# Prompt attention of a streaming encoder step: masking on GpSimd, plain transposes, outputs normalised by queries

## The chip, the core and the metric

The kernel runs on one core of a Trainium2 chip. The time is the device time of one execution in microseconds (us). The core's engines work side by side: TensorE (PE; PEld is its weight load), VectorE (DVE), ScalarE (ACT), GpSimd (POOL) and SyncE (SP), which here issues the loads and stores. Each engine runs its own list of instructions in order, and they meet only at semaphores.

## The reference, cut to what matters

The program is one inference step of a two-layer encoder for one prompt of 512 rows and eight running streams of 16 new rows. The part of interest is the first layer's attention over the prompt, eight heads of 64 columns, with a bias made of a running sum c of forget values:

```python
def fox_block(q, k, v, cq, ck, qpos, kpos):
    s = jnp.einsum('bqhd,bkhd->bhqk', q, k).astype(jnp.float32) * (HEAD_DIM ** -0.5)
    bias = jnp.swapaxes(cq, 1, 2)[..., :, None] - jnp.swapaxes(ck, 1, 2)[..., None, :]
    mask = kpos[None, :] <= qpos[:, None]
    p = jax.nn.softmax(jnp.where(mask, s + bias, -jnp.inf), axis=-1)
    return jnp.einsum('bhqk,bkhd->bqhd', p.astype(v.dtype), v)

def fox_prompt(q, k, v, logf):
    ...
    for i in range(t_len // Q_BLOCK):
        lo, hi = i * Q_BLOCK, (i + 1) * Q_BLOCK
        outs.append(fox_block(q[:, lo:hi], k[:, :hi], v[:, :hi], c[:, lo:hi], c[:, :hi], pos[lo:hi], pos[:hi]))
```

A block of 128 queries sees the keys up to its own end; only the last 128 of these keys need the mask. The streams' attention (the same over 512 cached keys and 16 new ones, for each of eight streams) follows, then the layer's RWKV heads, and the feed-forward parts stand before and behind.

## The kernel before

The engines' lists are written by hand, one function per engine and stage, and called in a fixed order: no scheduler moves anything. Prompt attention is `pe_prompt`, `dve_prompt` and `act_prompt`, with `sp_streams` and `pool_streams` (loads and operands of the streams' attention) beside it.

There are 16 steps. `pstep(n)` gives step n its pair of heads p = n // 4 and its tile of 128 queries qt = n % 4; the step has kl = 128 (qt + 1) keys, so the steps of a pair grow: 128, 256, 384, 512 keys. Scores are negated (q is scaled by a negative factor), so that the row minimum plays the part of the maximum. A step goes through these operations, for both heads of the pair (h = 0, 1):

- `scores` (TensorE, L1154): queries times keys into banks b and b + 1 of PSUM, then (L1157) a product of the identity and `causal` (0 or 1e30) added to the last 128 columns.
- `biased` (VectorE, L1110): adds `c_rows`, the forget sums of the pair's heads as rows that stand on all partitions, writes `prob` and the row minimum `nmax`. `c_rows` lies in `norm_buf`, 512 columns for each head.
- `exponentials` (ScalarE, L1083): in place, with the row sums into `esum`.
- `diagonals` (VectorE, L1118, L1120): the reciprocal of the sums, and the identity times it (`sum_diag`).
- `turn` (TensorE, L1167): each 128x128 block of `prob` times `sum_diag`, which turns and normalises it, into banks 4 and 5. ScalarE copies head 0 (L1101) and VectorE head 1 (L1143) to `prob_t` in `pair_raw`.
- `outputs` (TensorE, L1179): v of one head as weights (64 columns) times the turned block (128 columns), summed over the key blocks. The result has the head's columns on partitions and the queries on columns, in bank 6 or 7.
- ScalarE rounds it into `act_hi` (L1092), VectorE writes the rest into `act_lo` (L1136). These are the operands of the output projection.

The loops interleave the steps. In iteration n TensorE issues `scores(n + 1)`, `outputs(n - 1)`, `turn(n)`; ScalarE `act_hi` of n - 1, `exponentials(n + 1)`, the copy of n; VectorE `biased(n + 1)`, `act_lo` of n - 1, the copy of n, `diagonals(n + 1)`. `prob` has two buffers, `prob_t` one.

The streams' attention begins once the last `act_lo` is written (`s_ol`). Its cached keys and values are loads of 1 MB, with two buffers each: the first lies in `yflat`, the second in `norm_buf`, keys on the forget rows of heads 0 to 3, values on those of heads 4 to 7. `sp_streams` issues the first stream's loads early, waits for the last `act_lo`, issues the second stream's, then the RWKV stage's loads (`sp_rwkv_loads`), and then for each further stream its keys, when the keys of two streams before have been turned (L1231), and its values, when the products of two streams before are done. GpSimd's `pool_streams` clears and fills `q_blocks` (on the same memory as `head_rows`) and copies the new keys while the prompt's steps run.

Of the kernel before, what the change touches and what calls it, by code (L numbers as in the profile page):

```python
# [157 lines left out]
def build(nc, io):  # L158
    ctx = ExitStack()
    with ctx:  # L160
# [114 lines left out]
        sum_diag = [pair_raw[0][:, 4 + 2 * i:6 + 2 * i, :] for i in range(2)]  # L275
# [10 lines left out]
        def level_mask(lv):  # L286
# [60 lines left out]
        s_sc, s_bs, s_ex, s_rs, s_dg = (sem(n) for n in (  # L347
            "scores", "scores_with_bias", "exponentials", "row_sum_inverse", "sum_diagonals"))
# [722 lines left out]
        def pstep(n):  # L1071

            p, qt = divmod(n, 4)
            return p, qt, (qt + 1) * P, 2 * (n % 2)

        def act_prompt(act):
            def exponentials(n):
                p, qt, kl, b = pstep(n)
                for h in range(2):
                    act.wait_ge(s_bs, 2 * n + h + 1)  # L1080
                    if n >= 2:
                        act.wait_ge(s_dg, n - 1)
# [5 lines left out]
            for n in range(PSTEPS + 1):  # L1088
                if n >= 1:
                    p, qt, kl, b = pstep(n - 1)  # L1090
                    act.wait_ge(s_o, n)
                    act.activation(act_hi[:, p, qt * P:(qt + 1) * P], ps[:, 6 + (n - 1) % 2, 0:P], ACT.Copy)\  # L1092
                       .then_inc(s_oh, 1)
# [9 lines left out]
        def dve_prompt(dve):  # L1103
            def biased(n):
                p, qt, kl, b = pstep(n)
                for h in range(2):
                    dve.wait_ge(s_sc, 2 * n + h + 1)
                    if n >= 2:
                        dve.wait_ge(s_pt, 2 * (n - 1))
# [5 lines left out]
            def diagonals(n):  # L1115
                b = pstep(n)[3]
                dve.wait_ge(s_ex, 2 * n + 2)
                dve.reciprocal(rsum[:, b:b + 2], esum[:, b:b + 2]).then_inc(s_rs, 1)  # L1118
                dve.wait_ge(s_rs, n + 1)
                dve.tensor_tensor(sum_diag[n % 2], ident[:, :].rearrange("p (o c) -> p o c", o=1)  # L1120
                                  .broadcast_to([P, 2, P]),
                                  rsum[:, b:b + 2].rearrange("p (h o) -> p h o", o=1).broadcast_to([P, 2, P]),
                                  ALU.mult).then_inc(s_dg, 1)
# [4 lines left out]
            diagonals(0)  # L1128
            for n in range(PSTEPS + 1):
                if n + 1 < PSTEPS:  # L1130
                    biased(n + 1)
                if n >= 1:
                    p, qt, kl, b = pstep(n - 1)
                    cols = slice(qt * P, (qt + 1) * P)
                    dve.wait_ge(s_oh, n)
                    dve.tensor_tensor(act_lo[:, p, cols], ps[:, 6 + (n - 1) % 2, 0:P],  # L1136
                                      act_hi[:, p, cols].bitcast(F32), ALU.subtract).then_inc(s_ol, 1)
                if n < PSTEPS:
# [4 lines left out]
                    dve.tensor_copy(prob_t[1][:, 0:kl], ps[:, 5, 0:kl]).then_inc(s_ptd, 1)  # L1143
                if n + 1 < PSTEPS:
                    diagonals(n + 1)

        def pe_prompt(pe):
            def scores(n):
# [3 lines left out]
                for h in range(2):  # L1152
                    rows = slice(64 * h, 64 * h + 64)
                    pe.matmul(ps[:, b + h, 0:kl], qk[rows, p, qt * P:(qt + 1) * P], qk[rows, 4 + p, 0:kl],  # L1154
                              start=True, stop=False)
                for h in range(2):
                    pe.matmul(ps[:, b + h, qt * P:kl], ident[:, :], causal, start=False, stop=True)\  # L1157
                      .then_inc(s_sc, 1)

            def turn(n):  # L1160
                p, qt, kl, b = pstep(n)
                pe.wait_ge(s_dg, n + 1)
                for h in range(2):
# [262 lines left out]

# [1486 lines left out]
```

## Time and profile before

| | us |
|---|---|
| median of 3 runs | 2772.81 (2771.42 to 2778.17) |
| the profiled execution | 2770.99 |
| its span | 2769.2 |
| TensorE busy | 2649.7 (96%) |
| VectorE busy | 1031.3 (37%) |
| ScalarE busy | 889.2 (32%) |
| GpSimd busy | 97.0 (4%) |

The span is what the profiler recorded of that execution, and the execution's own time lies 1.8 us above it. The steps of prompt attention are a small part of it, so shares over the span say little about them; they are read from the table of stretches and from the instructions in order of time. In a row of the timeline the first number is the start in us from the span's start, the second how long the merged instructions take together; "[... <-X]" is idle time of the engine ahead of it and who ended it. An f32 product shows as two records; a transpose of one 128x128 block as one.

### The profile page before, as it was taken

The page shows a single profiled execution, that of the slowest core. Times are in us where ns is not written, and L with a number is a line of the kernel's source. Part 1 is how long each engine was busy: PE and PEld are TensorE (multiplying, and loading weights), DVE is VectorE, ACT ScalarE, POOL GpSimd, SP SyncE. Part 2 cuts the span into 40 slices and gives each one's busy share as a digit, 9 for nine tenths or more (in the row PEclk, how much of TensorE's full clock was granted, in tenths as well). Part 3 has the DMA queues.
Part 4 walks back from the last instruction along what each step waited for, and adds up shares of the span by engine and source line. Part 5 has one row for each costly group of instructions (what it writes and reads, how often), then busy time and mean ns, then how long its engine had stood idle before and what let it go on. Part 6 is the DMA issues. An engine that isn't in the chain of part 4 may idle for free. (4 is left out here: it accounts for less than half of the span.)

```text
span 2769.2 us, 46298 instructions
## 1 busy us (share of the span) xinstructions
PE 2649.7 (96%) x19617; PEld 2414.5 (87%) x19617; DVE 1031.3 (37%) x1387; ACT 889.2 (32%) x1517; POOL 97.0 (4%) x88
## 2 busy tenths in 40 slices
PE   7999999999987988999999999999999989999998
PEld 7998997998656876899899899989979769989997
DVE  3232224332534764522232352222243364222234
ACT  4331223222334554432122343212233344321222
POOL 0000001000001221000000100000010010000001
PEclk9999999999899999999999999999999999999999
DMA  4221222221261003222222222312223222222222
GB/s 129 76 87 58 76 68 84 76 68 52 74 204 55 3 5 94 60 76 78 74 76 76 84 71 74 95 60 74 70 75 100 69 61 73 71 87 65 76 76 84
DMA packets 279809, 208.66 MB, mean 75 GB/s; under 512 B 24292, under 2 KB 236414, under 8 KB 279688
## 3 DMA queue, kind: packets, MB, share of 16 engines
q1 hardware_dynamic: 279688, 206.91, 24.9%
q8 instruction: 92, 1.51, 0.2%
q14 instruction: 29, 0.24, 0.0%
HBM read 199.85 MB, written 7.03 MB: 75 GB/s over the span
## 5 line engine op out<-in xcount | busy, mean ns | idle before, releaser
L449 PE MATMUL ps<-act_hi,pair_hi 128*128 128x320 f32 x2976 | 678.5, 309 | 0.6 <-DVE pair_lo L411 0.6
L449 PE MATMUL ps<-act_lo,pair_hi 128*128 128x320 f32 x2976 | 678.4, 309 | 0.0
L449 PE MATMUL ps<-act_hi,pair_lo 128*128 128x320 f32 x2976 | 677.3, 309 | 0.0
L449 PEld LDWEIGHTS ps<-act_hi,pair_lo 128*128 128x128 f32 x2976 | 497.8, 188 | 0.0
L449 PEld LDWEIGHTS ps<-act_lo,pair_hi 128*128 128x128 f32 x2976 | 497.8, 188 | 0.0
L449 PEld LDWEIGHTS ps<-act_hi,pair_hi 128*128 128x128 f32 x2976 | 496.7, 188 | 0.8 <-ACT qk L890 0.8
L411 DVE TENSOR_TENSOR pair_lo<-pair_raw,pair_hi 128x1024 fp32r<-128x1024 f32 x206 | 253.7, 1236 | 425.6 <-ACT pair_hi L407 425.6
L407 ACT ACTIVATE pair_hi<-pair_raw 128x1024 fp32r<-128x1024 f32 x206 | 215.9, 1053 | 457.6 <-PE ps L449 310.6
L485 PE MATMUL ps<-row_hi,hid_hi 128*128 128x512 f32 x880 | 345.8, 393 | 6.7 <-DVE row_lo L438 6.7
L485 PE MATMUL ps<-row_hi,hid_lo 128*128 128x512 f32 x880 | 344.4, 391 | 0.0
L485 PE MATMUL ps<-row_lo,hid_hi 128*128 128x512 f32 x880 | 344.3, 391 | 0.0
L430 ACT ACTIVATE row_hi<-row_raw 128x512 fp32r<-128x512 f32 x228 | 141.6, 630 | 404.3 <-DMA row_raw<-in_ffn_w_out_dram 274.0
L438 DVE TENSOR_TENSOR row_lo<-row_raw,row_hi 128x512 fp32r<-128x512 f32 x228 | 168.4, 752 | 247.6 <-ACT row_hi L430 247.1
L605 ACT ACTIVATE hid_hi<-hid 128x640 f32 (+1 forms) x88 | 65.1, 740 | 538.5 <-DVE hid L632 538.5
L632 DVE TENSOR_TENSOR hid<-silu,ps 128x640 f32<-128x640 f32 x88 | 72.3, 821 | 422.9 <-PE ps L449 413.1
L485 PEld LDWEIGHTS ps<-row_hi,hid_hi 128*128 128x128 f32 x880 | 165.1, 188 | 44.3 <-DVE row_lo L438 8.6
L485 PEld LDWEIGHTS ps<-row_lo,hid_hi 128*128 128x128 f32 x880 | 165.1, 188 | 36.8
L485 PEld LDWEIGHTS ps<-row_hi,hid_lo 128*128 128x128 f32 x880 | 165.2, 188 | 35.6
L485 PE MATMUL ps<-row_hi,act_hi 128*128 128x512 f32 x280 | 116.4, 416 | 17.6 <-DVE row_lo L438 16.6
L469 PE MATMUL ps<-act_hi,pair_hi 128*128 128x320 f32 x320 | 101.7, 318 | 18.5 <-DVE act_lo L749 13.0
L795 POOL TENSOR_TENSOR y<-y,norm_buf 128x512 f32<-128x512 f32 x30 | 44.1, 1504 | 2047.6 <-ACT norm_buf L676 2047.6
L485 PE MATMUL ps<-row_lo,act_hi 128*128 128x512 f32 x280 | 113.3, 405 | 0.0
(383 smaller groups left out, 2562.8 us busy)
## 6 DMA issues: line engine op xcount, KB each, us to landing
pair_raw<-in_ffn_w_in_dram SPq DMA_DIRECT2D x176, 512.0 KB, 3.8
row_raw<-in_ffn_w_out_dram SPq DMA_DIRECT2D x176, 256.0 KB, 2.9
pair_raw<-in_even_w_in_dram SPq DMA_DIRECT2D x22, 512.0 KB, 3.8
norm_buf<-in_norm_g_dram SPq DMA_DIRECT2D x12, 512.0 KB, 4.3
y<-in_cache_fox_k_dram SPq DMA_DIRECT2D x4, 1024.0 KB, 7.6
y<-in_cache_fox_v_dram SPq DMA_DIRECT2D x4, 1024.0 KB, 6.7
norm_buf<-in_cache_fox_k_dram SPq DMA_DIRECT2D x4, 1024.0 KB, 7.7
norm_buf<-in_cache_fox_v_dram SPq DMA_DIRECT2D x4, 1024.0 KB, 5.4
```

The source lines that it names most:

```text
L407: act.activation(pair_hi[c][:, :, :], pair_raw[c][:, :, :], ACT.Copy).then_inc(s_pair_hi[c], 1)
L411: dve.tensor_tensor(pair_lo[c][:, :, :], pair_raw[c][:, :, :], pair_hi[c][:, :, :].bitcast(F32), ALU.subtract).then_inc(s_pair_lo[c], 1)
L430: act.activation(row_hi[i % n][:, :], raw, ACT.Copy).then_inc(s_row_hi, 1)
L438: dve.tensor_tensor(row_lo[i % n][:, :], raw, row_hi[i % n][:, :].bitcast(F32), ALU.subtract).then_inc(s_row_lo, 1)
L449: mm = pe.matmul(ps[:, 2 * c + h, 0:HALF], w[c][:, k, :], a[:, k, h * HALF:(h + 1) * HALF], start=(k == 0 and w is pair_hi and a is act_hi ...
L469: mm = pe.matmul(ps[:, 2 * c + h, 0:HALF], w[c][:, k, :], a[:, k, h * HALF:(h + 1) * HALF], start=(k == 0 and w is pair_hi and a is act_hi ...
L485: mm = pe.matmul(ps[:, bank, :], a[:, k, t * P:(t + 1) * P], w[i % n][:, :], start=(k == 0 and w is row_hi and a is left_hi), stop=(k == k ...
L605: act.activation(halves(hid_hi, j), hid[:, :, :], ACT.Copy).then_inc(s_hid_hi, 1)
L632: dve.tensor_tensor(hid[:, :, :], silu[:, :, :], wide(2), ALU.mult).then_inc(s_pair_read[1], 1)
L795: pool.tensor_tensor(y[:, t, 0:512], y[:, t, 0:512], g_post[:, 0:512], ALU.mult).then_inc(s_yg[0], 1)
```

## The change

**Masking.** The two mask products of each step are gone. GpSimd adds `causal` to the last 128 columns of the pair's forget rows, in place, before the step's `biased` reads them. So that the mask may stay there, a pair's query tiles run from the last to the first: 512, 384, 256, 128 keys. Each mask but a pair's first waits until the previous step's bias has been added, and `biased` waits for it (`s_mask`). The streams' operands are made between masks.

**Turning.** `turn` is a plain transpose of each block and waits for the exponentials, not for a diagonal. `sum_diag` is gone; `inverse` only takes the reciprocal.

**Outputs.** The turned block is now the weights (128 columns) and v of one head streams (64 columns); the result has the queries on partitions. VectorE multiplies it by the reciprocal sums (`normalised`, into `fox_out`), TensorE transposes that (`turn_out`) into the same bank's next 128 columns, and from there `act_hi` and `act_lo` are read. VectorE's `act_lo` now stands behind its copy of the turned probabilities.

**Loads.** The second stream's keys wait for eight steps of bias (`s_bs` at 16), its values for all sixteen (32), not for the last `act_lo`.

```diff
@@ pstep @@
-            return p, qt, (qt + 1) * P, 2 * (n % 2)
+            return p, 3 - qt, (4 - qt) * P, 2 * (n % 2)
@@ act_prompt @@
                     if n >= 2:
-                        act.wait_ge(s_dg, n - 1)
+                        act.wait_ge(s_rs, n - 1)
...
-                    act.wait_ge(s_o, n)
-                    act.activation(act_hi[:, p, qt * P:(qt + 1) * P], ps[:, 6 + (n - 1) % 2, 0:P], ACT.Copy)\
+                    act.wait_ge(s_ot, n)
+                    act.activation(act_hi[:, p, qt * P:(qt + 1) * P], ps[:, 6 + (n - 1) % 2, P:2 * P], ACT.Copy)\
                        .then_inc(s_oh, 1)
@@ dve_prompt @@
                     dve.wait_ge(s_sc, 2 * n + h + 1)
+                    dve.wait_ge(s_mask, n + 1)
...
-            def diagonals(n):
+            def inverse(n):
                 b = pstep(n)[3]
                 dve.wait_ge(s_ex, 2 * n + 2)
+                if n >= 2:
+                    dve.wait_ge(s_on, n - 1)
                 dve.reciprocal(rsum[:, b:b + 2], esum[:, b:b + 2]).then_inc(s_rs, 1)
+
+            def normalised(n):
+                b = pstep(n)[3]
+                dve.wait_ge(s_o, n + 1)
                 dve.wait_ge(s_rs, n + 1)
-                dve.tensor_tensor(sum_diag[n % 2], ident[:, :].rearrange("p (o c) -> p o c", o=1)
-                                  .broadcast_to([P, 2, P]),
-                                  rsum[:, b:b + 2].rearrange("p (h o) -> p h o", o=1).broadcast_to([P, 2, P]),
-                                  ALU.mult).then_inc(s_dg, 1)
+                if n >= 2:
+                    dve.wait_ge(s_ot, n - 1)
+                dve.tensor_tensor(fox_out[n % 2].rearrange("p (h c) -> p h c", h=2),
+                                  ps[:, 6 + n % 2, 0:P].rearrange("p (h c) -> p h c", h=2),
+                                  rsum[:, b:b + 2].rearrange("p (h o) -> p h o", o=1).broadcast_to([P, 2, HEAD]),
+                                  ALU.mult).then_inc(s_on, 1)
...
                 if n >= 1:
-                    p, qt, kl, b = pstep(n - 1)
...
+                    normalised(n - 1)
                 if n < PSTEPS:
...
                     dve.tensor_copy(prob_t[1][:, 0:kl], ps[:, 5, 0:kl]).then_inc(s_ptd, 1)
+                if n >= 1:
+                    lo(n - 1)
                 if n + 1 < PSTEPS:
-                    diagonals(n + 1)
+                    inverse(n + 1)
@@ pe_prompt @@
                     pe.matmul(ps[:, b + h, 0:kl], qk[rows, p, qt * P:(qt + 1) * P], qk[rows, 4 + p, 0:kl],
-                              start=True, stop=False)
-                for h in range(2):
-                    pe.matmul(ps[:, b + h, qt * P:kl], ident[:, :], causal, start=False, stop=True)\
-                      .then_inc(s_sc, 1)
+                              start=True, stop=True).then_inc(s_sc, 1)
...
-                pe.wait_ge(s_dg, n + 1)
                 for h in range(2):
+                    pe.wait_ge(s_ex, 2 * n + h + 1)
                     if n:
                         pe.wait_ge(s_ptd if h else s_pta, n)
                     for k in range(qt + 1):
-                        mm = pe.matmul(ps[:, 4 + h, k * P:(k + 1) * P], prob[n % 2][h][:, k * P:(k + 1) * P],
-                                       sum_diag[n % 2][:, h, :], start=True, stop=True)
+                        mm = pe.transpose(ps[:, 4 + h, k * P:(k + 1) * P], prob[n % 2][h][:, k * P:(k + 1) * P],
+                                          ident[:, :])
...
-                for k in range(qt + 1):
-                    for h in range(2):
-                        mm = pe.matmul(ps[64 * h:64 * h + 64, 6 + n % 2, 0:P],
-                                       vtok[:, k, p * P + 64 * h:p * P + 64 * h + 64],
-                                       prob_t[h][:, k * P:(k + 1) * P], start=(k == 0), stop=(k == qt))
+                for h in range(2):
+                    for k in range(qt + 1):
+                        mm = pe.matmul(ps[:, 6 + n % 2, 64 * h:64 * h + 64], prob_t[h][:, k * P:(k + 1) * P],
+                                       vtok[:, k, p * P + 64 * h:p * P + 64 * h + 64], start=(k == 0), stop=(k == qt))
                 mm.then_inc(s_o, 1)
+
+            def turn_out(n):
+                pe.wait_ge(s_on, n + 1)
+                pe.transpose(ps[:, 6 + n % 2, P:2 * P], fox_out[n % 2], ident[:, :]).then_inc(s_ot, 1)
...
                 if n < PSTEPS:
                     turn(n)
+                if n >= 1:
+                    turn_out(n - 1)
@@ sp_streams @@
                 if b == 1:
-                    sp.wait_ge(s_ol, PSTEPS)
+                    sp.wait_ge(s_bs, PSTEPS)
...
+                if b == 1:
+                    sp.wait_ge(s_bs, 2 * PSTEPS)
@@ pool_streams, now pool_prompt_and_streams @@
+            def mask(n):
+                p, qt, kl, b = pstep(n)
+                if n % 4:
+                    pool.wait_ge(s_bs, 2 * n)
+                if n % 4 == 0:
+                    pool.wait_ge(s_cra, p + 1)
+                    pool.wait_ge(s_crd, p + 1)
+                at = c_rows[:, 2 * p:2 * p + 2, qt * P:kl]
+                pool.tensor_tensor(at, at, same(causal, 2), ALU.add).then_inc(s_mask, 1)
```

The masks stand in GpSimd's list as 0 to 3, the clearing of `q_blocks`, 4 and 5, four of its copies (head 0), 6, four more (head 1), 7 and 8, the two copies of the new keys and forget values, 9 to 15.

TensorE, inside a pair: scores of the next step, outputs of the step before, turning of this step (here one with 384 keys in both). Before:

```order
L1154 MATMUL ps<-qk 128x512 [waits scores_with_bias]
L1154 MATMUL ps<-qk 128x512
L1157 MATMUL ps<-att_const,ident 128x128 x2
L1179 MATMUL ps<-pair_raw,vtok 64x128 [waits fox_lo,prob_t_by_dve,prob_t_by_act]
L1179 MATMUL ps<-pair_raw,vtok 64x128 x3
L1167 MATMUL ps<-pair_raw,xn_buf 128x128 [waits prob_t_by_act,sum_diagonals]
L1167 MATMUL ps<-pair_raw,xn_buf 128x128 x2
L1167 MATMUL ps<-pair_raw,xn_buf 128x128 [waits prob_t_by_dve]
L1167 MATMUL ps<-pair_raw,xn_buf 128x128 x2
```

TensorE at the same place now (L1169 scores, L1191 outputs, L1179 turning, L1197 the output's transpose):

```order
L1169 MATMUL ps<-qk 128x256 [waits scores_with_bias]
L1169 MATMUL ps<-qk 128x256
L1191 MATMUL ps<-vtok,pair_raw 128x64 [waits fox_lo,prob_t_by_dve,prob_t_by_act]
L1191 MATMUL ps<-vtok,pair_raw 128x64 x7
L1179 MATMUL ps<-ident,xn_buf 128x128 [waits prob_t_by_act,exponentials]
L1179 MATMUL ps<-ident,xn_buf 128x128 x2
L1179 MATMUL ps<-ident,xn_buf 128x128 [waits prob_t_by_dve,exponentials]
L1179 MATMUL ps<-ident,xn_buf 128x128 x2
L1197 MATMUL ps<-ident,pair_raw 128x128 [waits fox_normalised]
```

The mask products are gone, outputs have the form 128x64, and behind the turning stands a transpose of the outputs of the step before.

ScalarE, two iterations in the first pairs (L1092 act_hi, L1083 exponentials, L1101 the copy of turned probabilities). Before:

```order
L1092 ACTIVATE act_hi<-ps 128x128 [waits fox_out]
L1083 ACTIVATE xn_buf,esum<-xn_buf,nmax 128x384 [waits sum_diagonals,scores_with_bias] x2
L1101 ACTIVATE pair_raw<-ps 128x256 [waits fox_out,prob_turned]
L1092 ACTIVATE act_hi<-ps 128x128 [waits fox_out]
L1083 ACTIVATE xn_buf,esum<-xn_buf,nmax 128x512 [waits sum_diagonals,scores_with_bias] x2
L1101 ACTIVATE pair_raw<-ps 128x384 [waits fox_out,prob_turned]
```

ScalarE now:

```order
L1093 ACTIVATE act_hi<-ps 128x128 [waits fox_turned]
L1084 ACTIVATE xn_buf,esum<-xn_buf,nmax 128x256 [waits row_sum_inverse,scores_with_bias] x2
L1102 ACTIVATE pair_raw<-ps 128x384 [waits fox_out,prob_turned]
L1093 ACTIVATE act_hi<-ps 128x128 [waits fox_turned]
L1084 ACTIVATE xn_buf,esum<-xn_buf,nmax 128x128 [waits row_sum_inverse,scores_with_bias] x2
L1102 ACTIVATE pair_raw<-ps 128x256 [waits fox_out,prob_turned]
```

The order of the three is the same; `act_hi` waits for the output's transpose instead of the outputs.

SyncE's queue at the second stream's loads (keys, values, then the first of the RWKV loads). Before:

```order
L1216 DMA y<-in_cache_fox_v_dram 128x4x512
L1212 DMA norm_buf<-in_cache_fox_k_dram 128x4x512 [waits fox_lo]
L1216 DMA norm_buf<-in_cache_fox_v_dram 128x4x512
L1493 DMA rw_const<-in_rw_const_dram 128x836 [waits qk_new_set]
L1494 DMA reset_p<-in_rw_const_dram 128x512
```

The same place now:

```order
L1235 DMA y<-in_cache_fox_v_dram 128x4x512
L1229 DMA norm_buf<-in_cache_fox_k_dram 128x4x512 [waits scores_with_bias]
L1235 DMA norm_buf<-in_cache_fox_v_dram 128x4x512 [waits scores_with_bias]
L1529 DMA rw_const<-in_rw_const_dram 128x836 [waits qk_new_set]
L1530 DMA reset_p<-in_rw_const_dram 128x512
```

Nothing moved in the queue; the two waits are for bias steps instead of the last `act_lo`.

## Rows read from the trace of the kernel before

**Rows 1.** Table of stretches: pair 1 and pair 3 of prompt attention; columns in the head line.

```profile
core 0: us, PE busy (x) PEld busy (x) DVE busy (x) ACT busy (x) POOL busy (x), PEclk, DMA share, GB/s
715.60:731.65 16.05, 16.05 (x104) 11.88 (x104) 8.53 (x34) 7.57 (x27) 3.03 (x11) 0.82 0.01 2
745.21:758.77 13.56, 13.56 (x113) 10.15 (x112) 8.57 (x32) 6.85 (x24) 0.00 (x0) 1.00 0.01 2
```

**Rows 2.** Timeline at the stage's end: a copy, the outputs behind it, the streams' first products.

```profile
768.65 0.47 ACT L1101 ACTIVATE pair_raw<-ps 128x384 f32<-128x384 f32 x1
...
769.25 0.88 PE L1179 MATMUL ps<-pair_raw,vtok 128*64 128x128 f32 x12 [0.70 <-ACT pair_raw L1101]
...
774.72 1.96 PE L1231 MATMUL ps<-ident,y 128*128 128x128 f32 x16 [0.69 <-DVE act_lo L1136]
```

**Rows 3.** Timeline of TensorE alone inside pair 3 (start, us, what).

```profile
751.10 1.13 PE L1154 MATMUL ps<-qk 64*128 64x512 f32 x4
752.16 0.71 PE L1157 MATMUL ps<-att_const,ident 128*128 128x128 f32 x4
752.80 0.66 PE L1179 MATMUL ps<-pair_raw,vtok 128*64 128x128 f32 x8
753.39 1.60 PE L1167 MATMUL ps<-pair_raw,xn_buf 128*128 128x128 f32 x12
754.92 0.49 PE L1154 MATMUL ps<-qk 64*128 64x128 f32 x4
755.35 0.71 PE L1157 MATMUL ps<-att_const,ident 128*128 128x128 f32 x4
...
756.79 2.05 PE L1167 MATMUL ps<-pair_raw,xn_buf 128*128 128x128 f32 x16
758.77 0.49 PE L1154 MATMUL ps<-qk 64*128 64x256 f32 x2
```

**Rows 4.** Timeline of TensorE in the streams' attention: third, fourth and fifth key turn.

```profile
797.09 1.97 PE L1231 MATMUL ps<-ident,y 128*128 128x128 f32 x8 [5.78 <-DMA y<-in_cache_fox_k_dram]
...
806.11 1.09 PE L1231 MATMUL ps<-ident,norm_buf 128*128 128x128 f32 x8
...
814.17 1.09 PE L1231 MATMUL ps<-ident,y 128*128 128x128 f32 x8 [0.28 <-DMA y<-in_cache_fox_k_dram]
```

**Rows 5.** Timeline of SyncE's queue: second stream's values, RWKV states, third stream's keys.

```profile
775.11 0.51 SPq L1216 DMA_DIRECT2D norm_buf<-in_cache_fox_v_dram  x1
...
779.51 9.78 SPq L1501 DMA_DIRECT2D state_raw<-in_state_rwkv_dram  x8
789.34 0.62 SPq L1212 DMA_DIRECT2D y<-in_cache_fox_k_dram  x1
```

**Rows 6.** Lines L1003 (transposes) and L2447 (one streamed column): ns min/median/max, first and last start.

```profile
L1003 PE MATMUL ps<-ident,qk x20: 272/273/302, 690.3 to 692.4; 128*128 128x128 f32 x20
```

```profile
L2447 PE MATMUL ps<-ones,ln_g x16: 245/245/266, 2152.0 to 2153.7; 1*128 1x1 f32 x16
```

**Rows 7.** Timeline of ScalarE inside pair 3.

```profile
753.51 0.28 ACT L1092 ACTIVATE act_hi<-ps 128x128 fp32r<-128x128 f32 x1 [1.64 <-PE ps L1179]
753.68 0.71 ACT L1083 ACTIVATE xn_buf<-xn_buf,nmax 128x512 f32<-128x512 f32 x1
...
755.09 0.48 ACT L1101 ACTIVATE pair_raw<-ps 128x384 f32<-128x384 f32 x1
...
757.08 0.39 ACT L1083 ACTIVATE xn_buf<-xn_buf,nmax 128x128 f32<-128x128 f32 x1
...
757.99 0.60 ACT L1101 ACTIVATE pair_raw<-ps 128x512 f32<-128x512 f32 x1
```

**Rows 8.** Groups of GpSimd, shapes apart: busy us, mean ns, idle before.

```profile
L2304 POOL TENSOR_TENSOR norm_buf<-norm_buf,rw_const 128x512 f32<-128x512 f32 x8 | 10.2, 1273 | 54.7 <-DVE norm_buf L2134 46.4 <-PE ps L1781 4.4 <-DVE sig_g L1559 3.9
```

**Rows 9.** Table of stretches behind the late key load, and in the streams' last steps.

```profile
797.10:800.00 2.90, 2.90 (x14) 2.90 (x15) 0.21 (x1) 0.65 (x3) 0.00 (x0) 0.50 1.05 387
800.00:801.00 1.00, 1.00 (x10) 0.85 (x8) 0.64 (x3) 0.81 (x1) 0.00 (x0) 1.00 0.28 102
851.00:854.30 3.30, 1.49 (x17) 1.11 (x17) 2.26 (x9) 0.94 (x4) 0.00 (x0) 1.00 0.00 0
```

More of the change, by code:

```diff
@@ L274, in build @@
         prob_t = [pair_raw[h][:, 0:4, :].rearrange("p k c -> p (k c)") for h in range(2)]
-        sum_diag = [pair_raw[0][:, 4 + 2 * i:6 + 2 * i, :] for i in range(2)]
+        fox_out = [pair_raw[0][:, 4 + i, :] for i in range(2)]
         new_mask = yflat[:, 4096:5120].rearrange("p (b c) -> p b c", c=P)
@@ L346, in build @@
         s_cr, s_cra, s_crd = sem("c_rows"), sem("c_rows_by_act"), sem("c_rows_by_dve")
-        s_sc, s_bs, s_ex, s_rs, s_dg = (sem(n) for n in (
-            "scores", "scores_with_bias", "exponentials", "row_sum_inverse", "sum_diagonals"))
+        s_sc, s_bs, s_ex, s_rs, s_mask, s_on, s_ot = (sem(n) for n in (
+            "scores", "scores_with_bias", "exponentials", "row_sum_inverse", "diagonal_masked", "fox_normalised",
+            "fox_turned"))
         s_pt, s_pta, s_ptd, s_o, s_oh, s_ol = (sem(n) for n in (
@@ L1113, in biased, with lo @@
                                              accum_out=nmax[:, b + h:b + h + 1]).then_inc(s_bs, 1)
-            def diagonals(n):
+            def inverse(n):
                 b = pstep(n)[3]
                 dve.wait_ge(s_ex, 2 * n + 2)
+                if n >= 2:
+                    dve.wait_ge(s_on, n - 1)
                 dve.reciprocal(rsum[:, b:b + 2], esum[:, b:b + 2]).then_inc(s_rs, 1)
+            def normalised(n):
+                b = pstep(n)[3]
+                dve.wait_ge(s_o, n + 1)
                 dve.wait_ge(s_rs, n + 1)
-                dve.tensor_tensor(sum_diag[n % 2], ident[:, :].rearrange("p (o c) -> p o c", o=1)
-                                  .broadcast_to([P, 2, P]),
-                                  rsum[:, b:b + 2].rearrange("p (h o) -> p h o", o=1).broadcast_to([P, 2, P]),
-                                  ALU.mult).then_inc(s_dg, 1)
+                if n >= 2:
[4 more added lines that the diff above has]
+                                  ALU.mult).then_inc(s_on, 1)
+            def lo(n):
+                p, qt, kl, b = pstep(n)
+                cols = slice(qt * P, (qt + 1) * P)
+                dve.wait_ge(s_oh, n + 1)
+                dve.tensor_tensor(act_lo[:, p, cols], ps[:, 6 + n % 2, P:2 * P],
+                                  act_hi[:, p, cols].bitcast(F32), ALU.subtract).then_inc(s_ol, 1)
             dve.wait_ge(s_cra, FOXH // 2)
@@ L1127, in dve_prompt @@
             biased(0)
-            diagonals(0)
+            inverse(0)
             for n in range(PSTEPS + 1):
@@ L1132, in dve_prompt @@
                 if n >= 1:
-                    p, qt, kl, b = pstep(n - 1)
[L1134 to L1137, printed above, removed]
+                    normalised(n - 1)
                 if n < PSTEPS:
@@ L1408, in pool_fox_setup, with pool_prompt_and_streams, q_blocks_of @@
                                pattern=[[-FOXH, NSEQ], [-1, FOXH], [0, NEW]], channel_multiplier=1).then_inc(s_sel, 1)
-        def pool_streams(pool):
-            for c in range(2):
-                pool.wait_ge(s_pair_read[c], before("even_in", 0) + NQK + NRW + 1)
-            pool.wait_ge(s_cr, FOXH)
-            pool.memset(q_blocks, 0.0).then_inc(s_qb0, 1)
-            pool.wait_ge(s_qb0, 1)
-            for h in range(2):
+        def pool_prompt_and_streams(pool):
+            def mask(n):
+                p, qt, kl, b = pstep(n)
+                if n % 4:
[5 more added lines that the diff above has]
+                pool.tensor_tensor(at, at, same(causal, 2), ALU.add).then_inc(s_mask, 1)
+            def q_blocks_of(h):
                 rows = slice(64 * h, 64 * h + 64)
@@ L1420, in pool_streams @@
                                      qk[rows, p, SEQ:TOK].rearrange("p (b q) -> p b q", q=NEW)).then_inc(s_qb0, 1)
+            pool.wait_ge(s_att_const, 16)
+            for n in range(4):
+                mask(n)
+            for c in range(2):
+                pool.wait_ge(s_pair_read[c], before("even_in", 0) + NQK + NRW + 1)
+            pool.memset(q_blocks, 0.0).then_inc(s_qb0, 1)
+            mask(4)
+            mask(5)
+            pool.wait_ge(s_qb0, 1)
+            pool.wait_ge(s_mask, 6)
+            q_blocks_of(0)
+            pool.wait_ge(s_qb0, 5)
+            mask(6)
+            pool.wait_ge(s_mask, 7)
+            q_blocks_of(1)
             pool.wait_ge(s_qb0, 9)
+            mask(7)
+            mask(8)
             pool.wait_ge(s_logf, 1)
@@ L1425, in pool_streams @@
             pool.tensor_copy(k_new, qk[:, 4:8, SEQ:TOK]).then_inc(s_qkn, 1)
+            for n in range(9, PSTEPS):
+                mask(n)
         F4 = lambda a: a.rearrange("p (k c) -> p k c", k=4)
@@ L2759, in _ @@
             pool_fox_setup(pool)
-            pool_streams(pool)
+            pool_prompt_and_streams(pool)
             pool_rwkv_first(pool)
```

## The prediction

> **What bounds the kernel now.** The page shows one core with TensorE busy for 96% of 2769.2 us, so the first reading is where the edited work stands. By the table of stretches the sixteen steps of prompt attention begin at 715.60 us and the streams' attention at 774.72 [rows 1, 2]: 59.1 us of the span. In the middle, four steps (one pair of heads) take 13.56 us, and TensorE is busy for all of it, VectorE for 8.57 and ScalarE for 6.85 [rows 1]. TensorE's own rows have no idle note and follow each other without a gap: scores of 512 keys 1.06 us from start to start, the two mask products 0.64, outputs 0.59, turning 384 probabilities 1.53, turning 512 1.98 [rows 3]. So TensorE bounds this stretch, and the other engines have slack. Behind it the streams' third key load lands late: TensorE stands still for 5.78 us before 797.09 [rows 4]. The load was issued only at 789.34, 14.2 us after the issue at 775.11, with the RWKV loads in between, eight of which alone hold the queue for 9.78 us [rows 5].
>
> **What goes from TensorE.** The mask products: 0.64 us in each of 16 steps, 2.6 us per pair. The turning: between 384 and 512 keys two products more cost 0.45 us, so one f32 product of 128 columns costs 0.225 us and a step about 0.18 us beside it. A pair has 20 of them (two heads times 1+2+3+4 blocks), 20 x 0.225 + 4 x 0.18 = 5.2 us. A plain transpose costs 0.11 us: twenty start within 2.0 us [rows 6]. So 20 x 0.11 + 4 x 0.12 = 2.7 us, 2.5 us less.
>
> **What comes to TensorE.** Outputs by queries load 128 columns of probabilities as weights and stream only 64 columns of v. No row has that shape. Nearest are products with 128 weight columns and one streamed column: 16 records (two to a product) start within 1.7 us, 0.113 us each, as long as with 128 streamed columns [rows 3, 6]. I therefore take 0.225 us for each, 20 x 0.225 + 4 x 0.18 = 5.2 us per pair; before, outputs cost (0.59 us with two blocks) about 0.15 + 0.22 per block, 2.8 us per pair. If the streamed columns alone set the price, it would be half, 3.0 us; if load and product didn't overlap at all, 0.3 us a product, 6.8. I take 5.2, since the weight load is what these rows and the turning rows share. The output's own transpose adds 0.11 us in each step, and about 0.3 until ScalarE can read it. TensorE's own work per pair is then 3.0 (scores, 4 x 0.22 + 0.21 for each block) + 2.7 + 5.2 + 0.9 = 11.8 us in place of 13.56. If it alone bounded the stretch, that would save 7 us.
>
> **Why I don't take that saving.** The edit ties ScalarE into a ring. In its list the rounding copy into act_hi stands ahead of the next exponentials, and it now waits for the transposed output, which TensorE makes only after turning the probabilities. The next outputs wait for the copy that stands behind those exponentials. So from one outputs to the next everything is in series: outputs, turning, output transpose, act_hi, two exponentials, one copy, wake TensorE. Before, ScalarE's copy waited for outputs alone, and its exponentials ran beside the turning. Per pair: outputs 5.2; turning 2.7; output transpose till ScalarE starts 4 x 0.3 = 1.2; act_hi to exponential 4 x 0.17 = 0.7 [rows 7]; exponentials 0.39 us for 128 keys and 0.71 for 512, 0.5 and 0.6 between, two heads, 4.4 [rows 7]; copies 0.60 for 512 keys, 0.48 for 384, 0.37 and 0.26 by the same slope, 1.7 [rows 7]; from a copy's end (768.65 + 0.47) to TensorE's start at 769.25 0.13 us, four times 0.5 [rows 2]. Sum 16.4 us, 2.8 more than 13.56. The next scores lie in the ring's gap and are hidden. VectorE has 8.6 us of work per pair and fits: its normalising (0.3 us) lies beside the turning.
>
> **The end of the stage.** The first outputs start about where they did: scores of 512 and 384 keys at half clock take 3.8 us from 715.6, the first pair's mean granted clock of 0.82 puts the rise near 721 [rows 1], turning ends near 721.4, copy and wake 0.8: 722.4. Three pairs of 16.4 bring 771.6. Three steps to the last outputs are 4.8, 3.8 and 2.3 (a step's share of the ring; the last without 1.4 of exponentials): 782.5. Then the last tile: outputs 0.65, normalise 0.3, transpose 0.3, act_hi 0.3, act_lo 0.3, wake: 784.5. Before it was 774.72 [rows 2]. **The stage loses 9.8 us.**
>
> **GpSimd's masks.** Each adds 2 x 128 columns; a 128x512 addition on GpSimd takes 1.27 us [rows 8], so one takes at most that, probably 0.9. It waits until the previous step's bias has been added and is needed a ring turn later, 3.7 us at the shortest. Ahead of masks 6 and 7 it is queued behind four copies, 1.0 us. I put it at nothing; the cover is gone when mask and queue exceed about 2.4 us.
>
> **The queue of loads.** The second stream's keys now wait for the eighth step's bias and its values for the last step's bias, which come about 8 us ahead of the stage's end, since exponentials, turning, outputs and tail of two small tiles still follow. All that queues behind them moves too: the third key load is issued 14.2 - 8 = 6.3 us after the stage's end instead of 14.6, and lands 7.75 us later (797.09 - 789.34), at 14.1. TensorE wants it at 16.6 (791.31 - 774.72). So the wait of 5.78 goes, with 2.5 us to spare. Behind the wait the clock is 0.50 for 2.9 us [rows 9], and the key turn and its stream last 9.02 us where the next lasts 8.06 [rows 4]: 1.0 more. **Streams gain 6.8 us.** After that the loads set the same beat of 8 us; what is late next is again the key load behind v.
>
> **The sum.** 9.8 - 6.8 = +3.0 us. The profiled execution took 2770.99 us, so the sum gives 2774.0; the median of the runs lies 1.8 above it (2772.81), which gives 2775.8. I say 2775.
>
> **Rivals.** (a) Streamed columns set the price of outputs: the ring is 14.2 us per pair, the stage +1.2, in all -5.6: 2765.4, or 2767 against the median. For it: fewer columns; against it: the one-column products [rows 6]. 0.12. (b) The ring doesn't bind, TensorE's 11.8 us a pair do: stage -7, streams -6.8, 2761. For it: if ScalarE's order let exponentials run ahead; against it: the list in the order shown. 0.07. (c) **Slower by the clock.** TensorE now idles about a quarter of the ring. If the granted clock falls to its lower level inside the stage, the ring's TensorE part (5.2 + 2.7 + 1.2) doubles, 9 us for each pair at half clock; one pair gives 2784, all four 2811. For it: the clock stood at 0.50 behind the 5.78 us stop. Against it: from 851.0 to 854.3 TensorE was busy for 1.49 of 3.30 us at full clock [rows 9], though it dropped afterwards; the ring is busier, without a stop over 1.3 us. It decides from one such drop. The Trainium skill (TensorE: Matmul & The Clock Gate, Part 4) has a rule that speaks for it: transposes don't count as busy for the clock. By it these turns would keep the clock down and this rival would come in. The trace disagrees so far: from 797.1 to 800 TensorE did nothing but transposes at 0.50, and from 800 on the clock was 1.00 [rows 9]. 0.12. (d) The early loads don't bring the third keys forward (SP blocked, landing later): +9.8, 2782 to 2783. The queue rows speak against it [rows 5]. 0.10. (e) The masks don't run ahead and hold VectorE: above 2.4 us each, some 0.5 us a step, 8 in all, 2783. 0.04.
>
> **How the numbers follow.** The forecast has 0.55; its own range is 2770 to 2780, since thirty-two small latencies in the ring may be off by 0.1 us each. About 0.3% (8.3 us) is what a measurement of this kernel can tell from no change: 2764.5 to 2781.1. Faster holds (b) and a little of (a): 0.09. Slower holds (c), (d), (e) and the upper edge of the forecast: 0.27. Within: 0.64. The range goes from 2766 (most of (a)) to 2786 (one pair of (c), outputs at 0.3 us a product); it leaves out (b) and the rest of (c).
>
> **What would show it.** In the changed profile: four steps at 16.4 us with TensorE idle before each outputs, released by ScalarE's copy; outputs at 0.45 us a block of both heads (0.22 refutes me); act_hi waiting for the output transpose; the stage ending near 784.5; no idle before the third key turn; the bias rows never waiting for GpSimd; granted clock 1.00 after 721. A period below 13.6 us would make the prediction wrong from its main step; a clock of 0.50 in the middle would make it wrong upwards.

## The result and the profile after

The changed kernel takes 2790.24 us (median of 4 runs, 2786.89 to 2793.83), the kernel before beside it 2772.45: a ratio of 1.0064, with a 95% interval from 1.0048 to 1.0080. It is slower by 17.8 us, and outside the range of the prediction, 2766 to 2786. The profiled execution took 2787.44 us with a span of 2785.7, 16.5 more than before.

Where the 16.5 us lie, by the starts of three rows (first scores, first key turn, fourth key turn; before 715.60, 774.72, 806.11; after 712.19, 791.46, 818.89): the stage began 3.4 us earlier, lasted 79.3 instead of 59.1 (+20.2), the streams' first three turns took 27.4 instead of 31.4 (-4.0), and all that follows 1966.8 instead of 1963.1 (+3.7).

The table of stretches shows first what went wrong. These are the three parts of the stage behind its first pair in the changed kernel: pair 2, pair 3, and pair 4 with the tail (us, busy time of PE, PEld, DVE, ACT and POOL, then the granted clock). Their counterpart in the kernel before is in [rows 1].

```profile
core 0: us, PE busy (x) PEld busy (x) DVE busy (x) ACT busy (x) POOL busy (x), PEclk, DMA share, GB/s
726.20:742.70 16.50, 12.55 (x81) 8.74 (x80) 8.37 (x33) 6.74 (x24) 5.58 (x14) 0.91 0.05 7
742.70:765.30 22.60, 20.38 (x83) 15.11 (x82) 8.33 (x33) 6.74 (x24) 2.85 (x4) 0.50 0.11 43
765.30:791.46 26.16, 20.61 (x98) 14.37 (x97) 10.60 (x40) 8.77 (x33) 2.17 (x3) 0.63 0.33 104
```

A pair takes 16.5 us at nearly full clock, as the ring's sum said (16.4), and 22.6 at 0.50. A clock of 0.50 in the table is TensorE's lower level (1.2 in place of 2.4 GHz), so the time spent there is twice what a stretch's clock lacks to 1, times its length: 3.0 + 22.6 + 19.4 = 45 us of these 65.

The ring itself, in the timeline of TensorE and ScalarE with the clock at 1.00: outputs, turning, the output's transpose, act_hi, two exponentials, the copy, and the next outputs, which waited 1.30 us for that copy. The scores stand in the gap. In [rows 3, 7] the same operations ran side by side.

```profile
735.94 2.00 PE L1191 MATMUL ps<-vtok,pair_raw 128*128 128x64 f32 x16 [1.41 <-ACT pair_raw L1102]
...
737.78 0.83 PE L1179 MATMUL ps<-ident,xn_buf 128*128 128x128 f32 x6
...
738.44 0.27 PE L1197 MATMUL ps<-ident,pair_raw 128*128 128x128 f32 x1
...
738.64 0.49 PE L1169 MATMUL ps<-qk 64*128 64x128 f32 x4
738.75 0.28 ACT L1093 ACTIVATE act_hi<-ps 128x128 fp32r<-128x128 f32 x1 [2.86 <-PE ps L1197]
738.92 0.50 ACT L1084 ACTIVATE xn_buf<-xn_buf,nmax 128x256 f32<-128x256 f32 x1
...
739.42 0.49 ACT L1084 ACTIVATE xn_buf<-xn_buf,nmax 128x256 f32<-128x256 f32 x1
...
739.91 0.48 ACT L1102 ACTIVATE pair_raw<-ps 128x384 f32<-128x384 f32 x1
...
740.43 1.55 PE L1191 MATMUL ps<-vtok,pair_raw 128*128 128x64 f32 x12 [1.30 <-ACT pair_raw L1102]
```

Eight output products take 1.84 us from their start to the start of what follows (735.94 to 737.78), 0.23 each with 64 streamed columns. That is what f32 products with the same 128 weight columns and 128 streamed ones cost in the kernel before (0.225, turning in [rows 3]), so the streamed columns don't set the price. One pair later the same eight took 3.46 us, at the clock of 0.50:

```profile
754.58 3.67 PE L1191 MATMUL ps<-vtok,pair_raw 128*128 128x64 f32 x16 [0.88 <-ACT pair_raw L1102]
758.04 1.49 PE L1179 MATMUL ps<-ident,xn_buf 128*128 128x128 f32 x6
```

GpSimd's sixteen masks took 0.73 us each and were never late: no bias step waited for one. The timeline row of one, released by the step's bias before it:

```profile
733.41 0.73 POOL L1438 TENSOR_TENSOR norm_buf<-norm_buf,att_const 128x256 f32<-128x256 f32 x1 [1.81 <-DVE nmax L1112]
```

In the streams the wait of [rows 4] is gone. SyncE's queue issued the second stream's values 9.5 us ahead of the stage's end, and the third key turn stood ready; the rows are SyncE's and TensorE's timelines.

```profile
781.91 0.37 SPq L1235 DMA_DIRECT2D norm_buf<-in_cache_fox_v_dram  x1
...
795.16 0.39 SPq L1229 DMA_DIRECT2D y<-in_cache_fox_k_dram  x1
```

```profile
791.46 3.67 PE L1250 MATMUL ps<-ident,y 128*128 128x128 f32 x16 [0.69 <-DVE act_lo L1139]
...
810.67 1.09 PE L1250 MATMUL ps<-ident,y 128*128 128x128 f32 x8
...
818.89 1.09 PE L1250 MATMUL ps<-ident,norm_buf 128*128 128x128 f32 x8 [0.44 <-DMA norm_buf<-in_cache_fox_k_dram]
```

But the streams inherit the low clock: the first key turn takes 3.67 us where it took 1.96 [rows 2], and the third begins 19.2 us after the stage's end, not 16.6.

### The profile page after: what moved, and what is told of

The parts are those of the page before. It is cut to its first block and busy times, and to the rows that moved or that the text cites. A ratio compares the mean times of both kernels' runs of the same rounds, so it can differ in the third digit from the quotient of the medians.

```text
span 2785.7 us, 46113 instructions
## 1 busy us (share of the span) xinstructions
PE 2660.3 (95%) x19489; PEld 2420.7 (87%) x19489; DVE 1029.9 (37%) x1387; ACT 888.2 (32%) x1517; POOL 108.8 (4%) x104
## 5 line engine op out<-in xcount | busy, mean ns | idle before, releaser
L470 PE MATMUL ps<-act_hi,pair_hi 128*128 128x320 f32 x320 | 101.8, 318 | 18.5 <-DVE act_lo L750 13.0
L486 PE MATMUL ps<-row_hi,act_lo 128*128 128x512 f32 x280 | 113.7, 406 | 0.0
```

The source lines that it names most:

```text
L470: mm = pe.matmul(ps[:, 2 * c + h, 0:HALF], w[c][:, k, :], a[:, k, h * HALF:(h + 1) * HALF], start=(k == 0 and w is pair_hi and a is act_hi ...
L486: mm = pe.matmul(ps[:, bank, :], a[:, k, t * P:(t + 1) * P], w[i % n][:, :], start=(k == 0 and w is row_hi and a is left_hi), stop=(k == k ...
```

## The experiments

**Theories.** The ring was measured close to its forecast and the early loads as forecast, so the question is the clock. Three causes were set against each other: the outputs stream only 64 columns behind each weight load (T, thin work); TensorE waits in the ring (I, idle); transposes do not count as work for the clock, as the Trainium skill says (R; TensorE: Matmul & The Clock Gate, Part 4). T+I is the first two together. In the table, the stage is from the first scores to the streams' first key turn, and low clock is 2 x (1 - granted clock) x length, summed over the stage from the second pair on (every kernel starts its first pair at the lower level). The medians are of 10 runs in x3, x4, x6 and x9, 8 in x1, x5 and x8, 4 in the changed kernel and x10, 3 in x7 and 2 in x2. The kernel before ran beside each group and its median moved from 2772.2 to 2775.3, so kernels are best compared by the ratio; it is worked out from all runs and need not be the quotient of two medians. Stage, clock and period are of one profile each.

| kernel | stage us | low clock us | period of pair 3 us | median us | ratio to before (95%) |
|---|---|---|---|---|---|
| before | 59.1 | 0 | 13.56 | | 1 |
| changed | 79.3 | 45 | 22.6 | 2790.24 | 1.0064 (1.0048 to 1.0080) |
| x1 outputs stream 128 columns | 68.0 | 3 | 15.8 | 2778.67 | 1.0023 (1.0011 to 1.0035) |
| x8 filler in the gap | 68.1 | 0 | 16.1 | 2776.22 | 1.0016 (1.0003 to 1.0030) |
| x2 turning by products | 84.1 | 22 | 18.5 | 2787.87 | 1.0054 (1.0034 to 1.0075) |
| x10 transposes twice | 83.9 | 27 | 20.4 | 2793.31 | 1.0053 (1.0034 to 1.0073) |
| x3 exponentials first | 52.6 | 0 | 11.9 | 2765.37 | 0.9984 (0.9969 to 0.9999) |
| x9 exponentials first, 128 columns | 53.1 | 0 | 12.0 | 2760.38 | 0.9954 (0.9941 to 0.9968) |
| x4 early loads alone | 59.9 | 0 | 13.6 | 2767.24 | 0.9978 (0.9963 to 0.9994) |
| x5 masks alone | 55.6 | 0 | 12.3 | 2767.97 | 0.9983 (0.9972 to 0.9995) |
| x6 masks and early loads | 55.1 | 0 | 12.3 | 2764.19 | 0.9965 (0.9951 to 0.9979) |
| x7 changed, late loads | 81.0 | 36 | 16.5 | 2796.40 | 1.0085 (1.0056 to 1.0114) |

**x11, the changed kernel again.** No edit.

> The changed kernel again, for one more profile. If the drop of the clock belongs to the changed stage and not to one execution, it falls to 0.50 for 25 us or more between 720 and 790 again and the stage lasts 76 to 82 us; if it was chance, the stage lasts about 68 us.

One execution, 2791.94 us: stage 81.0 us, 36 us of low clock behind the first pair, nearly all of it in one piece at the end. The place differs from the first profile: there the whole of pair 3, here pair 4 and, before it, the whole first pair (17.9 us at 0.50). Over the whole stage the low clock is 49 us there and 54 here. The table of stretches, pair 3 and the rest:

```profile
747.88:764.34 16.46, 12.44 (x82) 8.63 (x81) 8.25 (x33) 6.73 (x24) 2.85 (x4) 0.91 0.14 55
764.34:794.39 30.05, 24.82 (x98) 18.37 (x97) 10.52 (x40) 8.76 (x33) 2.18 (x3) 0.50 0.35 100
```

So the fall belongs to this stage, not to one execution.

**x1, outputs stream 128 columns.** In `outputs`, with the rows that read it moved along (normalise takes head 0 from columns 0 to 63 and head 1 from 192 to 255, the transpose goes to 384 to 511):

```diff
-                        mm = pe.matmul(ps[:, 6 + n % 2, 64 * h:64 * h + 64], prob_t[h][:, k * P:(k + 1) * P],
-                                       vtok[:, k, p * P + 64 * h:p * P + 64 * h + 64], start=(k == 0), stop=(k == qt))
+                        mm = pe.matmul(ps[:, 6 + n % 2, P * h:P * h + P], prob_t[h][:, k * P:(k + 1) * P],
+                                       vtok[:, k, p * P:p * P + P], start=(k == 0), stop=(k == qt))
```

> Outputs load the same weights but stream both heads' v (128 columns in place of 64; the half that is not wanted is computed and left), which at full clock should cost nothing, since 128 weight columns set the price. In the changed kernel the granted clock fell to 0.50 for 34 us inside the stage, which lasted 79.3 us (712.2 to 791.5). Theory T (thin work: the clock follows how much TensorE streams, and 64 columns behind each weight load are too few): clock 1.00 through pairs 2 to 4, period 16.6 us, stage about 70, total 10 us less. Theory R (transposes do not count as work for the clock) and theory I (TensorE's waits of 1.3 us in the ring lower it): no change, stage 77 to 81.

Outputs of eight products took 1.89 us from start to start (changed: 1.84), the waits stayed, and the clock stayed up through pairs 2 and 3. TensorE's rows, then pair 3 and pair 4 with the tail in the table of stretches:

```profile
750.97 2.05 PE L1194 MATMUL ps<-vtok,pair_raw 128*128 128x128 f32 x16 [1.41 <-ACT pair_raw L1102]
752.86 0.82 PE L1182 MATMUL ps<-ident,xn_buf 128*128 128x128 f32 x6
...
755.51 1.60 PE L1194 MATMUL ps<-vtok,pair_raw 128*128 128x128 f32 x12 [1.30 <-ACT pair_raw L1102]
```

```profile
741.96:757.76 15.80, 11.50 (x82) 8.46 (x81) 8.20 (x33) 6.74 (x24) 2.86 (x4) 1.00 0.16 57
757.76:780.20 22.44, 14.96 (x97) 10.84 (x97) 10.28 (x40) 8.77 (x33) 2.18 (x3) 0.93 0.34 110
```

The streamed columns that nobody reads took 11.3 us off the stage and 11.6 off the median. T is right here; neither I nor R would have it, since waits and transposes are the same. The mean clock over a whole execution says so too: 0.980 to 0.987 in x1's eight runs, 0.974 to 0.978 in the changed kernel's five. But the clock isn't held to the end. In the last 3 us of the stage, from the last outputs on, it fell here as well, and the first key turn took 3.64 us as in the changed kernel.

**x8, filler in the gap.** Ahead of each `outputs`:

```diff
+                    for i in range(4):
+                        pe.matmul(ps[:, 6 + (n - 1) % 2, 3 * P:4 * P], ident[:, :], ident[:, :], start=True, stop=True)
                     outputs(n - 1)
```

> Four products of the identity with itself (128 columns each, 0.9 us in all at full clock, into unused columns of the outputs' bank) stand ahead of each step's outputs, in the stretch where TensorE waits for ScalarE's copy; nothing reads them. If the clock is the missing cost (T or I): clock 1.00, period 16.6 to 17, stage about 70, in spite of more work. If the ring itself was mis-sized and the clock only a companion: stage 79 or more, by up to 0.9 us a step.

```profile
742.47:758.55 16.08, 15.39 (x113) 12.07 (x113) 8.20 (x33) 6.74 (x24) 2.86 (x4) 1.00 0.16 59
```

Sixty-four products more, 14.0 us less in the median: TensorE busy for 15.39 of 16.08 us, clock 1.00, and here up to the streams, whose first key turn took 1.97 us. With the outputs as thin as in the changed kernel, filling the gap is enough too. So it took the two together, thin outputs and idle gaps, and repairing either holds the clock through the pairs. The filler also streams 128 columns a product, so x8 doesn't tell idle time from too little work streamed in all; a single cause of that kind would fit x1 and x8 alike.

**x2, turning by products.** `pe.transpose(..., ident)` becomes `pe.matmul(..., ident, start=True, stop=True)`.

> The probabilities are turned by a product with the identity instead of a transpose (0.225 us a block in place of 0.11, 2.5 us per pair more at full clock); all else as changed. Theory R (transposes do not count): clock 1.00, period 19.0 us, stage about 77. Theory T and theory I: the outputs and the waits stay, so the clock still falls; TensorE's part of the ring at half clock, stage 85 to 95.

**x10, transposes twice.** Each transpose is issued twice into the same place.

> Each block of probabilities is transposed twice into the same place, which takes as long as the product with the identity did (2.2 us per pair more). With products in place of transposes the granted clock was low for 24 us between 727 and 800, where the changed kernel had 51 us. Theory T+I (the clock follows how densely TensorE streams, whatever the kind of work): the same as with products, stage 80 to 88, low clock for 15 to 35 us of it. Theory R (transposes do not count): low throughout as in the changed kernel or more, with TensorE's 14.4 us a pair at half clock, stage 90 or more.

The two take the same time on TensorE (eight blocks 2.00 and 1.91 us) and differ only in the kind of work. Pair 2 and pair 3 of x2, then of x10:

```profile
729.85:749.55 19.70, 16.13 (x101) 12.46 (x100) 8.14 (x32) 6.74 (x24) 5.58 (x14) 0.86 0.04 10
749.55:768.00 18.45, 14.32 (x101) 11.42 (x101) 8.33 (x33) 6.74 (x24) 2.86 (x4) 0.95 0.13 48
```

```profile
730.14:750.07 19.93, 15.80 (x101) 12.72 (x100) 8.34 (x33) 6.73 (x24) 5.57 (x14) 0.87 0.09 24
750.07:770.50 20.43, 16.52 (x102) 12.87 (x101) 8.18 (x33) 6.73 (x24) 2.85 (x4) 0.83 0.08 29
```

Stages of 84.1 and 83.9 us, low clock for 22 and 27 us (33 and 33 with the first pair). By R the second would have stood at 0.50 throughout and the first at 1.00. T and I had expected 85 to 95 us for x2's stage and T+I 80 to 88 for x10's. More work of either kind shortened the low time (from 45) and neither ended it. These runs contradict the Trainium skill's rule for f32 transposes; x1 and x8 have them too, at a clock of 1.00.

**x3, exponentials first.** `act_hi` goes behind the copy, and `act_lo` behind the reciprocal (lines in parentheses stand for the operation's own lines):

```diff
@@ act_prompt @@
-                if n >= 1:
-                    (act_hi of step n - 1)
                 if n + 1 < PSTEPS:
                     exponentials(n + 1)
                 if n < PSTEPS:
                     (copy of step n)
+                if n >= 1:
+                    (act_hi of step n - 1)
@@ dve_prompt @@
-                if n >= 1:
-                    lo(n - 1)
                 if n + 1 < PSTEPS:
                     inverse(n + 1)
+                if n >= 1:
+                    lo(n - 1)
```

> ScalarE's order becomes exponentials of the next step, copy of the turned probabilities, act_hi of the step before; VectorE's act_lo goes behind the reciprocal. That cuts the ring: outputs, turning and one copy remain in series, about 12.5 us per pair at full clock. Theory I (waits lower the clock): TensorE is busy for 95%, clock 1.00, stage 54 to 58 us, total about 2760. Theory T: the clock still falls to 0.50, TensorE's 11.9 us a pair come near 20, stage 65 to 78, total 2772 to 2786.

```profile
738.54:750.47 11.93, 11.25 (x82) 8.30 (x81) 7.66 (x33) 7.14 (x25) 2.87 (x4) 1.00 0.25 85
```

The ring is cut: 11.93 us a pair, TensorE busy for 11.25 of them, stage 52.6, 6.5 shorter than before. That is the gain that the transposes and GpSimd's masks had to give, and the changed kernel's own order kept it from them. T alone expected the clock to fall here; with the gaps gone it stayed at 1.00 to the stage's end in this profile. But the profile is of the fastest of ten runs, which go from 2757 to 2779, and the median is only just clear of the kernel before.

**x9, x3 with the outputs of x1.**

> ScalarE's order of x3_exp_first together with the outputs that stream 128 columns. x3 had a stage of 52.6 us at full clock in its profile, but runs from 2757 to 2779. Theory T (thin streaming puts the clock at risk in some executions): runs lie close together at 2757 to 2762, since the clock no longer falls. If the spread comes from other stages' clock, it stays as wide and the median stays near 2765.

```profile
739.44:751.47 12.03, 11.39 (x81) 8.49 (x81) 7.66 (x33) 7.14 (x24) 2.86 (x4) 1.00 0.23 82
```

The profiled stage is no shorter than x3's, but the median is 5.0 us less and ten runs lie between 2755 and 2768 where x3's ten lie between 2757 and 2779. That fits T (in some executions of x3 the thin outputs still bring the clock down). The mean clock over a whole execution points the same way: 0.977 in x3's two longest runs (2775 and 2779 us), 0.982 to 0.987 in all ten of x9. No profile of a long execution of x3 shows where it fell, so it is not settled. x9 is the fastest kernel of the study and beats both: 13.1 us below the kernel before beside it (2773.48), ratio 0.9954.

**x4, early loads alone, and x7, the changed kernel without them.** The two waits of `sp_streams` in the kernel before, and taken out of the changed one.

> The kernel before with one part of the change alone: the second stream's keys wait for eight steps of bias, its values for sixteen. Nothing else moves. The last bias lies some 7 us ahead of the stage's end. Theory L (the prediction's): the third key turn starts 16.6 us after the stage's end instead of 22.4, without a wait, total 5 to 7 us less, about 2766. Rival (loads land later or the beat of 8 us gives it back): third key turn gains, later ones do not, total within 2 us of before. In the changed kernel the fourth key turn started 27.4 us after the stage's end, before 31.4, so at least 4 us should show.

> The changed kernel with the loads as before (both wait for the last act_lo). If the loads bring what the changed trace suggests (fourth key turn 27.4 us after the stage's end, before 31.4), it is 4 to 7 us slower than the changed kernel: about 2796. If the early loads are worth nothing, or disturb the stage, 2786 to 2792. The stage itself should stay at 77 to 81 us with the clock at 0.50 in its middle.

x4's queue and key turns (the stage ended at 772.89):

```profile
765.75 0.37 SPq L1218 DMA_DIRECT2D norm_buf<-in_cache_fox_v_dram  x1
...
779.27 0.62 SPq L1212 DMA_DIRECT2D y<-in_cache_fox_k_dram  x1
```

```profile
789.41 1.09 PE L1233 MATMUL ps<-ident,y 128*128 128x128 f32 x8
...
797.67 1.09 PE L1233 MATMUL ps<-ident,norm_buf 128*128 128x128 f32 x8 [0.48 <-DMA norm_buf<-in_cache_fox_k_dram]
```

The third key turn begins 16.5 us after the stage (forecast 16.6) and the fourth 24.8 instead of 31.4: 6.6 us less, forecast 6.8, and 6.2 less in the median. x7's median is 6.2 us above the changed kernel's, but with three and four runs the intervals of the two ratios overlap, so the gain on the changed kernel is not shown clear of noise. The stage of 81.0 us and 36 us of low clock came again in x7, without the early loads: they don't bring the clock down.

**x6, masks and early loads, and x5, masks alone.** The kernel before with `mask(n)`, the reversed tiles and no mask products; turning and outputs unchanged.

> The kernel before with GpSimd's masks, the reversed tile order and the early loads; turning stays a product with the diagonal and outputs keep their old form (64 weight columns, 128 streamed, no transpose of the output). It takes 2.6 us a pair from TensorE and closes no ring through ScalarE. By the terms of the prediction TensorE has 11.0 us a pair and the chain allows 12.2, so the stage lasts 52 to 54 us at full clock, and loads give 5 to 7 us more: total 2759 to 2762. Rival (the masks hold VectorE, or TensorE's clock falls here too): stage 57 or more, total 2765 or more.

> The kernel before with GpSimd's masks and the reversed tile order alone; loads, turning and outputs as before. With the early loads beside it the stage lasted 55.1 us (period 12.3) and the total was 9.3 us below before; early loads alone brought 6.2. So the masks alone should bring 3 to 5 us: stage about 55, total about 2769. If masks and loads overlap in what they give, it is under 2 us.

```profile
744.02:756.28 12.26, 11.27 (x98) 8.13 (x97) 8.31 (x32) 6.85 (x26) 2.87 (x4) 1.00 0.00 1
```

x5's pair takes 12.26 us. That is 1.3 less, of the 2.6 that the mask products were reckoned at; TensorE's busy time fell by 2.3 and it now waits for 1.0. The stage lasts 55.6 us, and the median is 7.3 us below the kernel before beside it; the ratio says 4.7, with an interval from 1 to 8. x6 is 9.3 us below. Its stage of 55.1 and median of 2764.19 missed the 52 to 54 and 2759 to 2762 expected. So masks and early loads each gain when nothing closes the ring, the masks about half of what they take from TensorE.

## Why the prediction was wrong, by its own steps

- **What bounds the kernel** held: TensorE in the stage before, the late key load behind it.
- **The terms of the ring** held. Output products cost 0.23 us each with 64 streamed columns, transposes 0.11, and a pair took 16.5 us in the changed kernel and 15.8 to 16.1 where the clock was 1.00, against 16.4. Outputs start up cheaper than I put it (1.84 us for eight products, not 1.98). The stage is 68.0 us in x1 and 68.1 in x8, 9 more than before; forecast 9.8.
- **GpSimd's masks** at nothing held: 0.73 us each, no bias step waited. **The loads** held: 6.6 of 6.8 us (x4). One difference there is off without effect: 14.2 - 8 is 6.2, and counted from the stage's end 6.6; in x4 the third keys were issued 6.4 us after it.
- **The step that failed is the clock**, rival (c), which I gave 0.12, and whose price at one pair (2784) I took as the range's end beside the costs of outputs. Measured, it took 11.3 us of the stage (79.3 against 68.0 in x1) and more behind it: the low clock ran on into the streams, whose fourth key turn came 4.0 us earlier in place of 6.6. 2775 + 11.3 + 2.6 is 2789, and the median is 2790. Against x8, where the clock stayed up to the streams, it is 11.2 in the stage and 2.5 in the streams (fourth key turn 27.4 against 24.9 us behind the stage's end), 13.7 of the 14.0 between the medians. x1 gets only 0.9 of these 2.5 back, since its clock fell at the stage's end too.
- Its price was set too high for each pair and counted for too few. The prediction doubled TensorE's part of the ring, 9 us for a pair at half clock. Pair 3, all of it at 0.50, took 22.6 us against 16.1 in x8, 6.5 more: part of the slower work went into what had been the gap.
- Within that step the error is in the argument against it. From [rows 9] I took 3.3 us with TensorE busy for 45% at clock 1.00, and set the ring's 75% beside it, as if busy time counted alike whatever fills it. x1 shows that it doesn't: with about the same busy time and the same waits the clock holds through the pairs when the products stream 128 columns and falls when they stream 64. What I had noted as a mere price, that outputs now pay for 128 weight columns and stream 64, was also what made the work thin. Before, the same stage streamed 128 columns behind 64 weight columns and had no gap.
- **The Trainium skill's rule** led to the right rival by a wrong road. The clock fell, but not for the transposes: x10 and x2 had much the same low time. The row against the rule [rows 9] was read rightly.
- The chances: 0.12 for (c) rested on a single stretch of other work. The range took in one pair at half clock (2784) while the text priced all four at 2811; the measured 45 us of low clock behind the first pair are the length of two to three pairs. Rival (b), which x3's order brings in, is summed wrongly: 13.8 us below 2772.8 is 2759, not 2761 (x9: 2760.38).

What follows the fourth key turn is the same code in all kernels but took from 1962.4 us (x3) to 1970.1 (x10) in the profiles, and the stage began between 712.2 and 717.7. The granted clock dips there at different places from one execution to the next: x11's page shows two dips, near 1050 to 1120 and 2230 to 2300 us, that the same kernel's first profile hasn't. So 3 to 4 us of a single profile's difference, such as the +3.7 and the -3.4 of the first table, can't be put down to an edit; the medians average over it.

## What to carry to other kernels

Ahead of moving a copy behind a new TensorE step, write down what stands behind that copy in its engine's list: here the next exponentials, and TensorE work that shrank from 13.56 us a pair to 11.25 (x3) became a ring that cost 2.9 us more; with the exponentials ahead of the copy the same operations took 11.9 us a pair instead of 16.5. When a product becomes bound by its weight load and gaps open beside it, look at TensorE's clock as a cost of its own; streaming columns that nobody reads, at 0.05 us for eight products, was worth 11 us here. And of a change with several parts, time the parts alone: here the early loads gained 6.2 us by themselves and the masks 4.7 to 7.3.

## What the runs showed of the hardware

- f32 products with 128 weight columns take 0.23 us each whether 64 or 128 columns stream (1.84 and 1.89 us for eight, after and x1).
- TensorE's clock fell to 0.50 for 36 to 45 us behind the first pair after the engine had been shown busy for 12.5 of 16.5 us a pair, and stayed there with 20.4 of 22.6 busy. About the same busy time with twice the streamed output columns kept it at 1.00 through pairs 2 and 3 (x1), filled gaps up to the streams (x8).
- Once low, the slower clock fills the gaps (busy 90% of pair 3, 76% of pair 2) and the profile's busy share looks healthy; only the clock column tells.
- f32 transposes and f32 products with the identity, at equal time, left the clock much alike (27 and 22 us low behind the first pair, 33 and 33 with it).
